# One shift of a value tile by one key: four partition ranges in place of two

## The chip, the cores and the metric

The kernel runs on one core of a Trainium2 chip. A core has TensorE (PE, with its weight loads PEld), VectorE (DVE), ScalarE (ACT), GpSimd (POOL), SyncE (SP) and 16 DMA engines, which move data between the chip's main memory and the on-chip memory of 128 partitions, or within the latter. The metric is the device time of one execution in microseconds, lower is better; each figure is a median of several executions.

## What is computed

Three blocks in a row on `x` of 512 tokens by 1024: a gated delta-rule layer, an attention layer with stick-breaking weights, and a block of a Fourier mixer beside dilated window attention. The change touches the second one. For each of 16 heads of width 64, with keys `k_sh` and values `v_sh`:

```
logits = einsum("bhtd,bhsd->bhts", q, kb) * Dh ** -0.5
mask = s_idx[None, :] < t_idx[:, None]
log_keep = where(mask, log_sigmoid(-logits), 0.0)
after = sum(log_keep, -1, keepdims=True) - cumsum(log_keep, -1)
wts = where(mask, exp(log_sigmoid(logits) + after), 0.0)
outs.append(einsum("bhts,bhsd->bhtd", wts, vb))
```

The kernel doesn't form `wts`. It runs a scan over the keys and multiplies its result by differences of neighbouring values, `v[s] - v[s-1]`. So each value row is needed once more, moved down by one key.

## The kernel before

All instructions of each engine are written out by hand in program order; nothing reorders them. Engines meet at semaphores only.

**Weights.** A dense product is cut into blocks of 512 output columns (`blocks`), a block into two halves `s`. SP loads a half (1 MB, 128 partitions) into `raw[:, s, :]` at L549. ACT rounds it into `whi` (L782), POOL subtracts the rounded part from `raw` and leaves the rest in `wlo` (L608), and PE computes hi·hi, lo·hi and hi·lo (L2072), three groups of 8 matmuls for each of the four output tiles of a block, two tiles to a half. The three products stand in for one of higher precision. There are two slots of `raw`, so SP may load a half of the next block only when POOL has finished with that of the block before (`raw_free` waits on `lo_ready`). The wait stands on SP, and everything that is written behind it on SP waits too.

**The stretch around the change.** The order of the blocks is `D_VB`, `D_VB + 1` (values, written by ACT into `Vb` at L1162 and L1146), `D_QB`, `D_QB + 1` (queries), `D_ZB`, `D_ZB + 1` (gate), then the attention. The names are indices of blocks. `Vb` is 128 partitions by `NT` = 4 by 1024 floats, token `128 * j + p` in partition `p` and row `j`; that is 16 KB in each partition.

**The shift.** Just ahead of the load of `D_ZB`, SP waits until `Vb` is complete and issues two transfers from `Vb` to `v_down`: partitions 0 to 126 go to partitions 1 to 127 (L590, 2032 KB), and partition 127 of rows 0 to 2 goes to partition 0 of rows 1 to 3 (L591, 12 KB). POOL clears the first key (L708). After both halves of `D_ZB` are split, POOL waits for `v_shifted` and subtracts `v_down` from `Vb` in four instructions (L713). The first reader of the differences is the attention, at L2710.

**What PE, ACT and DVE do at the same time.** For the queries, ACT squares each finished tile (L787), PE sums the squares over each head (`head_sums`, L2236), ACT takes the root (`root_pair`: L808, L809, L810, then L812, L814 into `rbuf`) and DVE scales (L1766). A `head_sums` waits until ACT has read the sums of the pair before (`ss_read`, counted up at L808 and L810). In ACT's program the rounding of the first half of `D_ZB` (`next_hi(D_QB + 1, 0)`) stands ahead of `roots(G_QB, SQ_QB)`. DVE copies finished query tiles out of the PSUM banks (L1756), which frees these banks for the tiles of `D_ZB`. ACT takes the gate tiles out at L1180 and L1185.

The five lines of PE's program in this stretch, in words: `dense_block(D_QB)`, `dense_unit(D_QB + 1, 0)`, a `head_sums`, `dense_unit(D_QB + 1, 1)` with a second `head_sums` between its two tiles, then the units of `D_ZB` in the same manner.

Of the kernel before, what the change touches and what calls it, by code (L numbers as in the profile page):

```python
# [104 lines left out]
def mixer_stack(nc, x, c, norm_g, w_ada, b_ada, w_in_a, conv_w_a, a_log_a, dt_bias_a, o_gain_a, w_out_a,  # L105
# [3 lines left out]
    with ctx:  # L109
        def sb(name, shape, dt=F32, scope=None):  # L110
            return (scope or ctx).enter_context(nc.sbuf_tensor(name, shape, dt))
# [99 lines left out]
        with ExitStack() as B:  # L211
# [4 lines left out]
            with ExitStack() as s2:  # L216
                v_down = sb("v_down", [128, NT, D], F32, s2)
# [15 lines left out]
            Vb = sb("Vb", [128, NT, D], F32, B)  # L233
# [74 lines left out]
        def raw_ch(s):  # L308
            return raw[:, s, :].rearrange("p (k n) -> p k n", k=KD)

        def spare(what, n):

            return what == "ada" and (n - EARLY) % 2 == 1
# [8 lines left out]
        def late_src(n, s):  # L322
            return late_w[:, s, :].rearrange("p (k n) -> p k n", k=KD) if spare("ada", n) else raw_ch(s)
# [15 lines left out]
        def early(u):  # L339

            return (ada_a if u % EARLY < 2 else ada_b)[:, u % 2 + 2 * (u // EARLY), :].rearrange("p (k n) -> p k n", k=KD)

        halves = [sum(kind == "t" for _, _, kind in blocks[:d]) for d in range(len(blocks))]

        def unit_used(eng, d, s):
# [9 lines left out]
        def unit(buf, s, kind):  # L355
            return buf[:, s, :].rearrange("p (k n) -> p k n", k=KD if kind == "ch" else KD // 2)
# [79 lines left out]
        def v_stage(n):  # L436

            return (pT2 if n in (6, 7) else yst if n in (2, 3, 10, 11) else vst)[:, n % 2, :]
# [86 lines left out]
        @block.sync  # L525
        def _(sp):
            def raw_free(r, s):

                of = [load for load in order[:r] if spare(*load) == spare(*order[r])]
                if not of:  # L530
                    sp.wait_ge(dense_full, 4 * D_OUTA)
                    return
                what, n = of[-1]
                sp.wait_ge(ada_done if what == "ada" else lo_ready, 2 * n + s + 1)

            def load(r, halves=(0, 1)):
                what, n = order[r]
                for s in halves:
                    if r:
                        raw_free(r, s)  # L540
                    if what == "dense" and blocks[n][2] == "t":
                        w, col, _ = blocks[n]
                        src = w[512 * s:512 * s + 512, col:col + 512].rearrange("(k p) n -> p k n", p=128)
                        dst = unit(raw, s, "t")
                    else:
                        w, col = ada[n] if what == "ada" else blocks[n][:2]
                        src = w[:, col + 256 * s:col + 256 * s + 256].rearrange("(k p) n -> p k n", p=128)
                        dst = late_src(n, s) if what == "ada" else raw_ch(s)
                    sp.dma_start(dst, src).then_inc((ada_loaded if spare(what, n) else raw_loaded)[s], 16)  # L549

            for i in range(NT):
                sp.dma_start(xnat[:, i, :], x[0, 128 * i:128 * i + 128, :]).then_inc(x_tile[i], 16)
            load(0, (0,))
            sp.wait_ge(rows_loaded, 16 * 13)
            for o, u in enumerate(EARLY_ORDER):
                if o == 2:
                    load(0, (1,))
                sp.dma_start(early(u), w_ada[0][:, 256 * u:256 * u + 256].rearrange("(k p) n -> p k n", p=128)
                             ).then_inc(ada_loaded[u], 16)
            sp.dma_start(cs[:, N_FIRST:N_CST], cst[:, N_FIRST:N_CST]).then_inc(cst_loaded, 16)  # L560
            with sp.Fori(1, 6) as i:
                for s in range(2):
                    sp.wait_ge(lo_ready, i * 2 + (s - 1))
                    src = w_in_a[0][:, bass.ds(i * 512 + 256 * s, 256)].rearrange("(k p) n -> p k n", p=128)
                    sp.dma_start(raw_ch(s), src).then_inc(raw_loaded[s], 16)
            def v_moves(n0, moves):

                for t in range(NT):
                    n = n0 + t
                    sp.wait_ge(v_done, 8 + n + 1)  # L570
                    for dst, src in moves(t, v_stage(n)):
                        sp.dma_start(dst, src).then_inc(v_moved[n % 2], 16)

            def moves_a(t, src):
                return [(vA[64:128, t, :], src[0:64, :]), (vA[0:64, t + 1, :], src[64:128, :])]

            def moves_b(cfg):
                return lambda t, src: [(vB[32 * t:32 * t + 32, r, cfg, :], src[r:128:4, :]) for r in range(NCLS)]

            for r in range(load_of["dense", 6], len(order)):  # L580
                if r == load_of["dense", D_VA2 + 2]:
                    sp.wait_ge(va_zero, 2)
                    v_moves(0, moves_a)
                if r == load_of["dense", D_VB2 + 2]:
                    sp.wait_ge(n_done, 4)
                    v_moves(4, moves_b(0))
                if r == load_of["dense", D_ZB]:
                    sp.wait_ge(v_done, 8)
                    sp.wait_ge(dense_full, 4 * (D_VB + 2))
                    sp.dma_start(v_down[1:128, :, :], Vb[0:127, :, :]).then_inc(v_shifted, 16)  # L590
                    sp.dma_start(v_down[0:1, 1:NT, :], Vb[127:128, 0:NT - 1, :]).then_inc(v_shifted, 16)  # L591
                load(r)
                if r == load_of["dense", D_VB2 + 2]:
                    v_moves(8, moves_b(1))
            sp.dma_start(picks_raw[:, :, :, :], pick.rearrange("a (n h m) -> a n h m", n=2, h=4)).then_inc(fc_loaded, 16)
            for b in range(2):
                for t in range(NT):
                    sp.wait_ge(out2_done, 4 * b + t + 1)
                    sp.dma_start(out[0, 128 * t:128 * t + 128, 512 * b:512 * b + 512],
                                 qB[:, 4 * b + t, :]).then_inc(stored, 16)  # L600
            sp.wait_ge(stored, 16 * 2 * NT)
# [3 lines left out]
        def _(pool):  # L605
            def split_lo(d, s):
                pool.wait_ge(hi_ready, 2 * d + s + 1)
                pool.tensor_tensor(wlo[:, s, :], raw[:, s, :], whi[:, s, :].bitcast(F32),  # L608
                                   ALU.subtract).then_inc(lo_ready, 1)
# [93 lines left out]
            for d in range(D_OUTA + 1, D_OUTB):  # L703
                for s in range(1 if d in own_parts else 2):
                    split_lo(d, s)
                if d == D_VB + 1:
                    pool.wait_ge(dense_full, 4 * (D_VB + 2))
                    pool.memset(v_down[0:1, 0, :], 0.0).then_inc(v_diff, 1)  # L708
                if d == D_ZB:
                    pool.wait_ge(v_diff, 1)  # L710
                    pool.wait_ge(v_shifted, 32)
                    for j in range(NT):
                        pool.tensor_tensor(Vb[:, j, :], Vb[:, j, :], v_down[:, j, :], ALU.subtract).then_inc(v_diff, 1)  # L713
            split_lo(D_OUTB, 0)
# [2319 lines left out]
```

## Time and profile before

| | us |
|---|---|
| median of 3 executions | 1237.84 (1235.95 to 1239.93) |
| profiled execution, its own time | 1238.93 |
| its span, first to last instruction | 1236.9 |
| PE busy | 1126.8 (91%) |
| PE weight loads busy | 887.0 (72%) |
| ACT busy | 520.1 (42%) |
| DVE busy | 498.2 (40%) |
| POOL busy | 381.3 (31%) |
| mean granted TensorE clock | 0.964 of full |

The program moves 119.37 MB by DMA, nearly all of it weights (the queue of SP and ACT, `q1` in the profile). The profile's views used here: the span in 40 slices (a digit is the busy share in tenths), the waits of an engine, the chain of work that ended last, the timelines of single engines, the view of one source line with its transfers' times from issue to landing, and sums over chosen stretches. Start times count from the span's start. A matmul's end is modelled, so starts of neighbours tell more than durations.

### The profile page before, as it was taken

The page shows a single profiled execution, that of the slowest core. Times are in us where ns is not written, and L with a number is a line of the kernel's source. Part 1 is how long each engine was busy: PE and PEld are TensorE (multiplying, and loading weights), DVE is VectorE, ACT ScalarE, POOL GpSimd, SP SyncE. Part 2 cuts the span into 40 slices and gives each one's busy share as a digit, 9 for nine tenths or more (in the row PEclk, how much of TensorE's full clock was granted, in tenths as well). Part 3 has the DMA queues.
Part 4 walks back from the last instruction along what each step waited for, and adds up shares of the span by engine and source line. Part 5 has one row for each costly group of instructions (what it writes and reads, how often), then busy time and mean ns, then how long its engine had stood idle before and what let it go on. Part 6 is the DMA issues. An engine that isn't in the chain of part 4 may idle for free.

```text
span 1236.9 us, 21346 instructions
## 1 busy us (share of the span) xinstructions
PE 1126.8 (91%) x8978; PEld 887.0 (72%) x8978; DVE 498.2 (40%) x889; ACT 520.1 (42%) x911; POOL 381.3 (31%) x153
## 2 busy tenths in 40 slices
PE   5999999999899999989018999999999999999998
PEld 4788876677678888767016766788887777678777
DVE  4575544544324382330013188284302333221553
ACT  4232237634246254531025488343324543653540
POOL 0143343132165214433016310123344222433161
PEclk8999999999999999989559999999999999999999
DMA  9723331486620222230212210132232512233301
GB/s 314 231 69 102 102 102 35 144 266 212 204 70 11 94 69 103 68 103 27 88 36 87 68 35 1 35 102 86 69 119 69 145 43 69 68 102 130 112 1 68
DMA packets 102976, 119.37 MB, mean 97 GB/s; under 512 B 4649, under 2 KB 89177, under 8 KB 102761
## 3 DMA queue, kind: packets, MB, share of 16 engines
q1 hardware_dynamic: 99024, 115.08, 28.8%
q10 hardware_dynamic: 3864, 3.01, 0.8%
q8 instruction: 68, 1.11, 0.4%
q14 instruction: 20, 0.16, 0.0%
HBM read 110.75 MB, written 2.10 MB: 91 GB/s over the span
## 4 chain that ended last, share of the span: by engine, by line
PE 77%; ACT 6%; another core or an unknown queue 5%; DVE 5%; issue 4%; DMA 1%; ACTq 0%; SPq 0%; POOL 0%; DVEq 0%
PE ps L2072 39%; PE ps L2865 4%; PE ps L2118 2%; PE ps L2213 2%; PE ps L2460 2%; PE ps L2675 2%; PE ps L2710 2%; PE ps L2156 1%; PE ps L2693 1%; PE ps L2831 1%; PE ps L2289 1%; PE ps L2487 1%; PE ps L2236 1%; PE ps L2818 1%
## 5 line engine op out<-in xcount | busy, mean ns | idle before, releaser
L608 POOL TENSOR_TENSOR wlo<-raw,whi 128x2048 fp32r<-128x2048 f32 x53 | 245.2, 4627 | 573.0 <-ACT whi L782 560.6
L782 ACT ACTIVATE whi<-raw 128x2048 fp32r<-128x2048 f32 x52 | 99.3, 1911 | 260.3 <-PE ps L2072 153.1
L614 POOL TENSOR_TENSOR wlo<-raw,whi 128x2048 fp32r<-128x2048 f32 x10 | 46.4, 4641 | 111.4 <-ACT whi L871 62.7
L2236 PE MATMUL ps<-work,cs 64*64 64x512 f32 x160 | 22.7, 637 | 57.0 <-ACT rbuf L810 57.0
L1802 DVE TENSOR_TENSOR_SCAN taken<-kept,taken 128x255 f32<-128x255 f32 (+2 forms) x64 | 51.2, 853 | 34.2 <-ACT taken L1202 34.1
L1292 ACT ACTIVATE p<-sc,nmx 128x256 f32<-128x256 f32 x64 | 32.0, 501 | 45.8 <-PE ps L2818 44.7
L1766 DVE SCALAR_TENSOR_TENSOR qTb<-qTb,qcol,rbuf 128x512 f32<-128x512 f32 x8 | 12.7, 1623 | 93.9 <-ACT rbuf L812 93.9
L2236 PEld LDWEIGHTS ps<-work,cs 64*64 64x64 f32 x160 | 4.4, 135 | 63.9 <-issue 63.1
L1899 DVE CUSTOM_DVE_ANT_0 sc<-ps,biast 128x256 f32<-128x256 f32 (+1 forms) x64 | 22.5, 393 | 65.8 <-PE ps L2807 36.7
L2072 PE MATMUL ps<-hC_hi,whi 128*128 128x512 f32 x184 | 47.0, 398 | 0.8 <-POOL wlo L608 0.8
L871 ACT ACTIVATE whi<-raw 128x2048 fp32r<-128x2048 f32 x11 | 21.1, 1917 | 62.7 <-PE ps L2072 62.7
L2072 PE MATMUL ps<-hC_lo,whi 128*128 128x512 f32 x184 | 45.5, 390 | 0.0
L2072 PE MATMUL ps<-hC_hi,wlo 128*128 128x512 f32 x184 | 45.5, 389 | 0.0
L2072 PEld LDWEIGHTS ps<-hC_hi,whi 128*128 128x128 f32 x184 | 33.7, 188 | 14.8 <-issue 6.4
L2072 PE MATMUL ps<-hB_hi,whi 128*128 128x512 f32 x120 | 35.1, 441 | 9.0 <-issue 5.6
L2072 PEld LDWEIGHTS ps<-hC_lo,whi 128*128 128x128 f32 x184 | 34.6, 188 | 7.4
L2072 PEld LDWEIGHTS ps<-hC_hi,wlo 128*128 128x128 f32 x184 | 34.6, 188 | 7.1
L2072 PE MATMUL ps<-hA_hi,whi 128*128 128x512 f32 x160 | 39.5, 389 | 0.0
L2072 PE MATMUL ps<-hA_hi,wlo 128*128 128x512 f32 x160 | 39.5, 390 | 0.0
L2072 PE MATMUL ps<-hA_lo,whi 128*128 128x512 f32 x160 | 39.5, 390 | 0.0
L2072 PEld LDWEIGHTS ps<-hB_hi,whi 128*128 128x128 f32 x120 | 25.1, 215 | 19.2 <-issue 13.8
L1470 DVE SCALAR_TENSOR_TENSOR work<-ps,cols,work 128x511 f32<-128x511 f32 (+1 forms) x48 | 36.0, 750 | 6.1 <-DVE work L1467 0.2
(506 smaller groups left out, 2714.9 us busy)
## 6 DMA issues: line engine op xcount, KB each, us to landing
raw<-in_w_in_dram SPq DMA_DIRECT2D x24, 1024.0 KB, 5.2
raw<-in_w_in_a_dram SPq DMA_DIRECT2D x16, 1024.0 KB, 5.6
raw<-in_w_ada_dram SPq DMA_DIRECT2D x8, 1024.0 KB, 5.1
late_w<-in_w_ada_dram SPq DMA_DIRECT2D x8, 1024.0 KB, 5.5
raw<-in_w_kv_dram SPq DMA_DIRECT2D x8, 1024.0 KB, 5.2
raw<-in_w_in_b_dram SPq DMA_DIRECT2D x8, 1024.0 KB, 5.6
ada_a<-in_w_ada_dram SPq DMA_DIRECT2D x4, 1024.0 KB, 9.9
ada_b<-in_w_ada_dram SPq DMA_DIRECT2D x4, 1024.0 KB, 13.2
```

The costliest lines, as they stand in the source:

```text
L608: pool.tensor_tensor(wlo[:, s, :], raw[:, s, :], whi[:, s, :].bitcast(F32), ALU.subtract).then_inc(lo_ready, 1)
L614: pool.tensor_tensor(wlo[:, s, :], raw[:, s, :], whi[:, s, :].bitcast(F32), ALU.subtract).then_inc(lo_ready, 1)
L782: A(whi[:, s, :], raw[:, s, :], ACT.Copy).then_inc(hi_ready, 1)
L1292: A(p2[:, n % 2, 256 * e:256 * e + 256], sc2[:, n % 2, 256 * e:256 * e + 256], ACT.Exp, scale=-1.0, bias=nmx[:, grp, t, 2 * hp + e:2 * hp ...
L1470: STT(y[:, n:], src[:, 0:T - n], tap(3 - n), y[:, n:], ALU.mult, ALU.add).then_inc(conv_step, 1)
L1802: last = dve.tensor_tensor_scan(taken[:, r % 3, keys], kept[:, r % 3, keys], taken[:, r % 3, keys], 0.0, ALU.mult, ALU.add)
L2072: last = mm(out, l[a], r[b], start=start and at == 0, stop=stop and at == n - 1)
L2118: last = mm(dense[m][:, cols], w[:, k, 128 * (m % 2):128 * (m % 2) + 128], x[:, k, cols], start=half == 0 and q == 0, stop=stop and q == 2 ...
L2213: last = mm(modrow(2 * EARLY)[32 * (k % 4):32 * (k % 4) + 32, :], cactz[:, k, 23 - n:55 - n], late_src(a, s)[:, k, :], start=n == 0 and k ...
L2236: last = mm(ssbank(g + tile)[to, :], ones[of, 0:64], work4[of, (n + tile) % 4, :], start=True, stop=True)
L2460: last = mm(block64(0, s, i, 1 - n), ntm[side(n), (2 * p + s) % 4, i, :], xin[side(n), (2 * p + s) % 4, i, :], start=True, stop=True)
L2865: last = mm(dense[2 * s + m], w[:, k, 128 * m:128 * m + 128], x[:, k, :], start=q == 0, stop=q == 23)
```

## The change

The first of the two transfers is written as three, over partitions 0 to 111, 112 to 119 and 120 to 126; the one of partition 127 stays as it is. POOL waits for 64 in place of 32, since each of the four transfers adds 16. The bytes moved, the place in SP's program and all else are the same.

```
                     sp.wait_ge(v_done, 8)
                     sp.wait_ge(dense_full, 4 * (D_VB + 2))
-                    sp.dma_start(v_down[1:128, :, :], Vb[0:127, :, :]).then_inc(v_shifted, 16)
+                    sp.dma_start(v_down[1:113, :, :], Vb[0:112, :, :]).then_inc(v_shifted, 16)
+                    sp.dma_start(v_down[113:121, :, :], Vb[112:120, :, :]).then_inc(v_shifted, 16)
+                    sp.dma_start(v_down[121:128, :, :], Vb[120:127, :, :]).then_inc(v_shifted, 16)
                     sp.dma_start(v_down[0:1, 1:NT, :], Vb[127:128, 0:NT - 1, :]).then_inc(v_shifted, 16)
...
-                    pool.wait_ge(v_shifted, 32)
+                    pool.wait_ge(v_shifted, 64)
```

## Rows read from the trace of the kernel before

**Rows 1.** The page, span in 40 slices of 30.9 us: granted TensorE clock

```profile
PEclk8999999999999999989559999999999999999999
```

**Rows 2.** Waits of PE, whole span: line, releaser: total us, times, longest

```profile
PE ps L2236 <- ACT rbuf L810: 57.0, 4, 56.5
...
PE ps L2072 <- ACT zsT L1180: 3.4, 1, 3.4
```

**Rows 3.** Chain that ended last, 560 to 680 us: start, length, what

```profile
580.59 59.13 another core or an unknown queue
```

**Rows 4.** Timeline of SP: start, length, line, operation, tiles, count

```profile
550.43 0.37 SPq L549 DMA_DIRECT2D raw<-in_w_in_b_dram  x1
550.90 0.80 SPq L590 DMA_DIRECT2D v_down<-Vb  x1
551.77 36.88 SPq L591 DMA_DIRECT2D v_down<-Vb  x1
...
588.69 9.60 SPq L549 DMA_DIRECT2D raw<-in_w_in_b_dram  x2
```

**Rows 5.** Line L549, loads issued in 550:551, then in 590:593

```profile
DMA to landing us min/median/max: 5.3/5.3/5.3
...
DMA to landing us min/median/max: 50.7/50.8/51.0
```

**Rows 6.** Stretches: engines' busy us (instructions), granted clock, DMA share, GB/s

```profile
548.00:550.00 2.00, 2.00 (x8) 1.53 (x6) 0.00 (x0) 0.00 (x0) 2.00 (x1) 0.62 1.05 370
...
556.00:558.00 2.00, 2.00 (x11) 1.65 (x10) 0.00 (x0) 0.00 (x0) 0.00 (x0) 1.00 0.06 25
...
612.00:614.00 2.00, 0.00 (x0) 0.00 (x0) 0.00 (x0) 0.00 (x0) 0.00 (x0) 0.50 0.06 25
...
642.00:644.00 2.00, 0.23 (x4) 0.26 (x8) 0.00 (x0) 1.94 (x4) 2.00 (x1) 0.50 0.00 0
```

**Rows 7.** Timeline of ACT; the bracket is idle time before and its releaser

```profile
639.74 1.91 ACT L782 ACTIVATE whi<-raw 128x2048 fp32r<-128x2048 f32 x1 [67.03 <-DMA raw<-in_w_in_b_dram]
...
642.95 0.68 ACT L810 ACTIVATE rbuf<-ps,cs 64x512 f32<-64x512 f32 x1
...
653.51 1.90 ACT L782 ACTIVATE whi<-raw 128x2048 fp32r<-128x2048 f32 x1
...
663.79 1.91 ACT L782 ACTIVATE whi<-raw 128x2048 fp32r<-128x2048 f32 x1 [7.34 <-PE ps L2072]
```

**Rows 8.** Timeline of PE (matmuls), 8 matmuls to a row

```profile
580.46 1.09 PE L2236 MATMUL ps<-work,cs 64*64 64x512 f32 x8
...
585.26 1.98 PE L2072 MATMUL ps<-hB_hi,wlo 128*128 128x512 f32 x8
643.77 1.99 PE L2236 MATMUL ps<-work,cs 64*64 64x512 f32 x8 [56.54 <-ACT rbuf L810]
...
652.61 2.02 PE L2072 MATMUL ps<-hB_hi,whi 128*128 128x512 f32 x8
...
663.62 1.09 PE L2236 MATMUL ps<-work,cs 64*64 64x512 f32 x8
...
670.32 1.09 PE L2236 MATMUL ps<-work,cs 64*64 64x512 f32 x8
...
680.51 3.75 PE L2072 MATMUL ps<-hB_hi,whi 128*128 128x512 f32 x8 [3.41 <-ACT zsT L1180]
684.06 2.94 PE L2072 MATMUL ps<-hB_lo,whi 128*128 128x512 f32 x8
```

**Rows 9.** Timelines of DVE (first two rows) and POOL (last two)

```profile
651.66 2.48 DVE L1756 COPY qTb<-ps 128x512 f32<-128x512 f32 x4
...
668.38 6.71 DVE L1766 SCALAR_TENSOR_TENSOR qTb<-qTb,qcol,rbuf 128x512 f32<-128x512 f32 x2 [14.25 <-ACT rbuf L812]
...
560.87 4.64 POOL L608 TENSOR_TENSOR wlo<-raw,whi 128x2048 fp32r<-128x2048 f32 x1 [10.47 <-ACT whi L782]
...
660.09 9.46 POOL L713 TENSOR_TENSOR Vb<-Vb,v_down 128x1024 f32<-128x1024 f32 x4
```

## Prediction

> **What bounds the kernel now.** Start with the page: TensorE is busy for 91% of the span, and its granted clock is near full in all slices but three in the middle [rows 1]. Next, the waits of PE. One stands out: a `head_sums` (L2236) waited for ACT's L810 for 57.0 us in four waits, 56.5 of it in one [rows 2]. The next one of interest is 3.4 us. A releaser is only the last link, so ask what ACT waited for. ACT's timeline says: the rounding of the first half of `D_ZB` (L782) started at 639.74 after 67.03 us idle, released by the DMA into `raw` [rows 7]. L810 stands behind it on ACT, and PE behind L810. The chain that ended last has the same hole: 59.13 us from 580.59 for which it knows only an unknown queue [rows 3]. So the question is why that load came so late.
>
> SP's timeline answers in part. The last load ahead of the shift went out at 550.43, the large shift transfer at 550.90 in 0.80 us, but the small one sat on SP from 551.77 for 36.88 us, so both loads of `D_ZB` went out only from 588.69 [rows 4]. And then they took 51 us to land, where the load issued at 550.43 took 5.3 [rows 5]. The stretches show what was going on: from 556 to 558 and from 612 to 614 us the DMA share is 0.06, one part in 16, at 25 GB/s, where with all engines at work it is 1.05 at 370 GB/s [rows 6]. One of 16 engines works, the rest are idle; by 642 it is over. The shift holds 2044 KB, 2.09 MB; at 25 GB/s that is 84 us, and from 551.8 to 639.7 there are 88 in which this engine also carries its shares of three loads. So the 127-partition transfer runs on a single DMA engine, each load behind it needs that engine for its own share (a load ends when its slowest share ends), and SP itself is held since that engine's queue is full.
>
> The Trainium skill, "DMA: Bandwidth & Descriptors", section "Why a DMA increments its semaphore by 16 and not by 1", has the rule for this: the number of engines is the largest one up to 16 that divides the slowest dimension of both sides, so 127 partitions go to one engine; the trace agrees by its share of 0.06 [rows 6]. By it 112 partitions take 16 engines, 8 take 8 and 7 take 7; no row here shows these three sizes.
>
> **The change, part by part.**
>
> 1. The 112 partitions. 112 x 16 KB is 1.84 MB. The upper bound of their time is one engine at 25 GB/s, 73 us; the lower bound is all at 370 GB/s, 5.0 us [rows 6]. I take 5.0: the loads of 128 partitions are the nearest row in shape, 112 is a multiple of 16 as 128 is, and 127 is a multiple of nothing.
>
> 2. The 8 and the 7 partitions. If each partition goes to an engine of its own, 16 KB at 25 GB/s is 0.7 us each. If all 15 go to one engine, 0.25 MB is 9.8 us. I take 1.3 for both and keep 9.8 as the bound.
>
> 3. Issue on SP. Between 0.37 us (a load) and 0.80 us (the large transfer) for each [rows 4], some 1 us more for two transfers added; the 36.88 goes, since no engine has a long backlog. These issues are hidden: after them SP waits anyway for POOL to free the slot, which is L608 at 560.87 plus 4.64, so 565.5 [rows 9]. The load ahead of the shift lands at 550.43 + 5.3 = 555.7. With 5.0 + 1.3 behind it the shift is over at about 562, and with 9.8 in place of 1.3 at 570.5.
>
> 4. The load of `D_ZB`, first half. Issued at 565.5, landed 5.3 later, at 570.8; in the bad case of step 3 at about 576. ACT wants it when PE has finished the second tile of `D_QB + 1`. At the same place a block later ACT starts 0.17 us after the `head_sums` (663.79 against 663.62) [rows 7, 8], so here at 580.46 + 0.17 = 580.63. Ten us to spare, 5 in the bad case. ACT's row moves from 639.74 to 580.63: **59.1 us earlier**.
>
> 5. What is late next. L810 ended at 642.95 + 0.68 = 643.63 [rows 7], now at 584.5. PE wants it for its second `head_sums`. One `head_sums` and one tile at full clock take 670.32 - 663.62 = 6.70 us [rows 8], so PE gets there at 587.16 and does not wait. The last query tile is done another 6.70 later, at 593.86, where `D_ZB` begins. It began at 652.61 [rows 8]: **58.75 us earlier**. Less than 59.1 because PE now has to do its own work in order, although the restart at half clock (1.99 for a `head_sums`, not 1.09 [rows 8]; clock 0.50 [rows 6]) is saved as well. For that start PE needs a free bank, so DVE's first copy of L1756. The four start at 651.66 and take 2.48 [rows 9]; 59.1 earlier the first ends at about 593.2, 0.7 before PE wants it. This is the tightest spot. If it is late by as much again, that costs 0.7.
>
> 6. POOL's subtraction (L713) started at 660.09 [rows 9] and moves to 601. The shift is over some 30 us before, also in the bad case, so the wait for 64 costs nothing. ACT's second rounding of `D_ZB` (653.51 [rows 7]) and POOL move by 59.1 with step 4. From 663 on the order of everything repeats with a common shift. The wait of PE before 680.51 for ACT's L1180 stays: behind it is DVE's L1766 at 668.38, 6.71 us for two [rows 9], which overlaps POOL's work and moves with POOL or with PE. So the shift of all that follows is between 58.75 and 59.1; I take 59.0.
>
> No later wait depends on an absolute time: loads are issued when a slot is freed, by the work before them.
>
> **The sum.** Span 1236.9 - 59.0 = 1177.9. Profiled execution 1238.93 - 59.0 = 1179.9. That execution lies 1.1 above the median of 1237.84, so the median should become 1178.8.
>
> **Rivals.**
>
> *A, the clock.* After 3.4 us idle PE restarted at 680.51 slowly: groups of 3.75 and 2.94 us in place of 1.98 [rows 8], 2.7 us lost. What it does there may depend on the idle stretch 36 us before, which goes. If the loss there goes as well, 1176.1. For it: nothing but that dependence. Against: at 548 the clock is also partly low (0.62) after a wait that came with no long hole before [rows 6]. The other way, one such restart more costs 2.7: 1181.5.
>
> *B, the 112 are not spread.* If they too go to one engine, the bytes on that engine are the same and so is the hole: 1237.8, no difference. The Trainium skill's "Rules for kernel authors" in "DMA: Bandwidth & Descriptors" speak against the change on their face: many small transfers should be merged, and two transfers over disjoint partition ranges bring nothing, since both use the same engines. Read so, the result would be B's. But that presumes that the one transfer is spread already, and a share of 0.06 says it is not [rows 6].
>
> *C, spread in part.* The transfer must be off the engines by 580.63 - 5.3 = 575.3, so 19.6 us after 555.7. At 25 GB/s an engine moves 0.49 MB in this, a fourth of 1.84: four engines are enough. With two it takes 36.7 us, the load lands near 597.7, 42 us earlier than now, and the time is 1195.8.
>
> *D, slower.* The 36.88 us on SP is a price of each transfer behind the first, not of the backlog. Then three such issues hold SP from 551.77 to 662.4, the load lands at 667.7 in place of 639.7, and the time is 1265.8. It decides from 28.8 us each: then the load lands 3.7 us later than now, which is 0.3%. For it: SP did stand for 36.88 with a 12 KB transfer. Against: 36.88 us at 25 GB/s is 0.92 MB, near half of the large one, so it looks like room made in a queue; and with nothing before them loads are issued in 0.37 [rows 4].
>
> **How the numbers follow.** The forecast 0.82, A 0.11 (both ways), C 0.02, B 0.03, D 0.02. The executions before spread by 2 us to either side. The range takes A both ways and that spread: 1176.1 - 2 = 1174 below, 1181.5 + 2 = 1183.5 above, which also holds the 0.7 of step 5. Faster by over 0.3% (3.7 us, about what a measurement of this kernel can tell from no change): forecast, A and C, 0.95. Same: B, 0.03. Slower: D, 0.02.
>
> **What would show it.** SP's loads of `D_ZB` at about 565.5 and 576.4, each landed in 5 to 6 us. DMA share from 556 to 562 near 1, not 0.06. ACT's L782 at 580.6, released by PE and not by DMA. No wait of PE for L810 above 1 us. The tile of `D_ZB` at 593.9, L713 near 601, and the same waits as before behind it, 59 us earlier; PE's clock at 1.00 from 590 to 620. I am wrong if SP still stands for tens of us behind L590, if one engine's share lasts beyond 575, or if a wait of PE of more than 3 us turns up between 587 and 650.

## The result and the profile after

The changed kernel takes 1180.67 us (median, 1178.48 to 1185.62) against 1238.58 for the kernel before in the same comparison: a ratio of 0.954, 95% interval 0.951 to 0.958. A second comparison on another chip, `e9_changed_again` below, gave 0.952 (0.951 to 0.954). The forecast was 1178.8 in a range of 1174 to 1183.5. The profiled execution took 1180.23 with a span of 1178.2, so 58.7 us of span less; 59.0 had been worked out.

From L593 on line numbers are two higher than before: L608 is now L610, L782 is L784, L713 is L715, L810 is L812, L1180 is L1182, L1756 is L1758, L1766 is L1768, L2072 is L2074 and L2236 is L2238. First the page: the two slices at 5 tenths of the clock in the middle are gone (compare [rows 1]; two slices at 8 remain), and PE is busy for 95% of the span.

```profile
PE 1123.5 (95%) x8978; PEld 883.7 (75%) x8978; DVE 496.7 (42%) x889; ACT 520.1 (44%) x911; POOL 381.6 (32%) x153
...
PEclk7899999999999999998999999999999999999999
```

PE's waits: the one of 56.5 us for L810 ([rows 2]) is no longer among them; what stood behind it in the list comes first now.

```profile
PE ps L2074 <- issue: 5.6, 1, 5.6
PE ps L2256 <- DMA cs<-in_cst_dram: 4.9, 1, 4.9
PE ps L2228 <- DMA ada_a<-in_w_ada_dram: 4.3, 3, 3.0
PE ps L2074 <- ACT zsT L1182: 3.3, 1, 3.3
```

SP's timeline (start, length), the answer to [rows 4]. The four transfers hold SP for 4.7 us in all, not 37.7, and the first load of `D_ZB` goes out at 566.82, when POOL has freed the slot.

```profile
551.39 1.43 SPq L590 DMA_DIRECT2D v_down<-Vb  x1
552.87 0.77 SPq L591 DMA_DIRECT2D v_down<-Vb  x1
553.70 0.78 SPq L592 DMA_DIRECT2D v_down<-Vb  x1
554.51 1.73 SPq L593 DMA_DIRECT2D v_down<-Vb  x1
566.82 36.02 SPq L549 DMA_DIRECT2D raw<-in_w_in_b_dram  x4
```

The two loads of `D_ZB` (issued in 566:568 and in 577:578) landed in about 6 us, where it was 51 ([rows 5]):

```profile
DMA to landing us min/median/max: 6.1/6.1/6.1
...
DMA to landing us min/median/max: 5.6/5.6/5.6
```

The stretches (last three columns: granted clock, DMA share, GB/s), beside [rows 6]. The shift has all engines up to about 561, half of the share to 564, and then it is nearly silent. The clock from 612 to 614 is 1.00, where it was 0.50.

```profile
556.00:558.00 2.00, 2.00 (x10) 1.65 (x10) 0.00 (x0) 0.00 (x0) 0.00 (x0) 1.00 1.08 288
558.00:560.00 2.00, 2.00 (x11) 1.65 (x10) 0.00 (x0) 0.00 (x0) 0.00 (x0) 1.00 1.07 319
...
562.00:564.00 2.00, 2.00 (x11) 1.65 (x10) 0.00 (x0) 1.10 (x3) 1.85 (x1) 1.00 0.48 83
564.00:566.00 2.00, 2.00 (x10) 1.66 (x9) 0.47 (x1) 0.00 (x0) 2.00 (x1) 1.00 0.03 3
...
612.00:614.00 2.00, 2.00 (x13) 0.80 (x12) 2.00 (x2) 0.00 (x0) 2.00 (x1) 1.00 0.00 0
```

ACT, PE and POOL beside [rows 7 to 9]. ACT's rounding of `D_ZB` at 581.91 is now released by PE (after 7.92 us idle) and not by the DMA; PE's second `head_sums` at 588.44 has no wait; the first tile of `D_ZB` starts at 595.05.

```profile
581.91 1.91 ACT L784 ACTIVATE whi<-raw 128x2048 fp32r<-128x2048 f32 x1 [7.92 <-PE ps L2074]
...
581.74 1.09 PE L2238 MATMUL ps<-work,cs 64*64 64x512 f32 x8
...
588.44 1.09 PE L2238 MATMUL ps<-work,cs 64*64 64x512 f32 x8
...
595.05 1.98 PE L2074 MATMUL ps<-hB_hi,whi 128*128 128x512 f32 x8
...
622.83 3.30 PE L2074 MATMUL ps<-hB_hi,whi 128*128 128x512 f32 x8 [3.34 <-ACT zsT L1182]
625.93 2.39 PE L2074 MATMUL ps<-hB_lo,whi 128*128 128x512 f32 x8
...
602.40 9.47 POOL L715 TENSOR_TENSOR Vb<-Vb,v_down 128x1024 f32<-128x1024 f32 x4
```

### The profile page after: what moved, and what is told of

It reads as the page before. It is cut to its first block, busy times and chain, and to the rows that moved or that the text cites. A ratio compares the mean times of both kernels' runs of the same rounds, so it can differ in the third digit from the quotient of the medians.

```text
span 1178.2 us, 21348 instructions
## 1 busy us (share of the span) xinstructions
PE 1123.5 (95%) x8978; PEld 883.7 (75%) x8978; DVE 496.7 (42%) x889; ACT 520.1 (44%) x911; POOL 381.6 (32%) x153
## 4 chain that ended last, share of the span: by engine, by line
PE 82%; ACT 7%; DVE 5%; issue 4%; DMA 1%; SPq 1%; ACTq 0%; POOL 0%; DVEq 0%
PE ps L2074 42%; PE ps L2867 4%; PE ps L2120 2%; PE ps L2462 2%; PE ps L2215 2%; PE ps L2677 2%; PE ps L2712 2%; PE ps L2158 1%; PE ps L2695 1%; PE ps L2291 1%; PE ps L2833 1%; PE ps L2489 1%; PE ps L2238 1%; PE ps L2820 1%; DMA ada_a<-in_w_ada_dram 1%
## 5 line engine op out<-in xcount | busy, mean ns | idle before, releaser
L610 POOL TENSOR_TENSOR wlo<-raw,whi 128x2048 fp32r<-128x2048 f32 x53 | 245.4, 4632 | 514.2 <-ACT whi L784 501.8
L784 ACT ACTIVATE whi<-raw 128x2048 fp32r<-128x2048 f32 x52 | 99.3, 1911 | 202.0 <-PE ps L2074 160.9
L2074 PE MATMUL ps<-hC_hi,whi 128*128 128x512 f32 x184 | 46.9, 397 | 0.8 <-POOL wlo L610 0.8
L2074 PE MATMUL ps<-hC_lo,whi 128*128 128x512 f32 x184 | 45.5, 390 | 0.0
L2074 PE MATMUL ps<-hC_hi,wlo 128*128 128x512 f32 x184 | 45.4, 389 | 0.0
L2074 PEld LDWEIGHTS ps<-hC_hi,whi 128*128 128x128 f32 x184 | 33.7, 188 | 14.8 <-issue 6.4
L2074 PE MATMUL ps<-hB_hi,whi 128*128 128x512 f32 x120 | 33.3, 424 | 8.9 <-issue 5.6
L2074 PEld LDWEIGHTS ps<-hC_lo,whi 128*128 128x128 f32 x184 | 34.5, 188 | 7.4
L2074 PEld LDWEIGHTS ps<-hC_hi,wlo 128*128 128x128 f32 x184 | 34.5, 188 | 7.2
L2074 PE MATMUL ps<-hA_lo,whi 128*128 128x512 f32 x160 | 39.5, 389 | 0.0
L2074 PE MATMUL ps<-hA_hi,wlo 128*128 128x512 f32 x160 | 39.5, 389 | 0.0
L2074 PE MATMUL ps<-hA_hi,whi 128*128 128x512 f32 x160 | 39.5, 389 | 0.0
L2074 PEld LDWEIGHTS ps<-hB_hi,whi 128*128 128x128 f32 x120 | 23.8, 203 | 17.8 <-issue 12.9
L1592 DVE COPY_PREDICATED yib<-cs,ps 128x256 f32<-128x256 int32 x20 | 10.0, 501 | 59.9 <-PE ps L2462 59.9
L625 POOL COPY yib<-cs 128x512 f32<-128x512 f32 x20 | 12.6, 630 | 70.1 <-PE ps L2490 70.1
L2074 PEld LDWEIGHTS ps<-hA_hi,wlo 128*128 128x128 f32 x160 | 30.0, 188 | 6.2
```

The costliest lines, as they stand in the source:

```text
L784: A(whi[:, s, :], raw[:, s, :], ACT.Copy).then_inc(hi_ready, 1)
L2074: last = mm(out, l[a], r[b], start=start and at == 0, stop=stop and at == n - 1)
```

## The experiments

**My theory:** the 127 partitions ran on one of 16 DMA engines, and each load behind them had to wait for that engine. **The rivals:** it is the hold of SP by the small transfer, not the engine; or only multiples of 16 are spread; or the number and the kind of the transfers matter by themselves. All differences below are against the changed kernel, except where said.

### The number of engines as a dose: 122, 123, 124, 126 partitions

The count of partitions sets the number of engines in my theory, so other splits of the same 127 give two, three, four and 14.

```
-                    sp.dma_start(v_down[1:113, :, :], Vb[0:112, :, :]).then_inc(v_shifted, 16)
-                    sp.dma_start(v_down[113:121, :, :], Vb[112:120, :, :]).then_inc(v_shifted, 16)
-                    sp.dma_start(v_down[121:128, :, :], Vb[120:127, :, :]).then_inc(v_shifted, 16)
+                    sp.dma_start(v_down[1:123, :, :], Vb[0:122, :, :]).then_inc(v_shifted, 16)
+                    sp.dma_start(v_down[123:128, :, :], Vb[122:127, :, :]).then_inc(v_shifted, 16)
...
-                    pool.wait_ge(v_shifted, 64)
+                    pool.wait_ge(v_shifted, 48)
```

The others differ in the bounds alone (123 and 4, 124 and 3, 126 and 1, each with the transfer of partition 127 as it was).

> The shift as 122, 5 and 1 partitions. My theory (a transfer's partitions are dealt out over as many engines as the largest divisor of their count up to 16, and the load behind waits for the slowest of them): 122 = 2 x 61 runs on two engines, DMA share 0.12 to 0.13 once the load ahead has landed, 1.0 MB each at 25 to 28 GB/s, over at 592 to 596. The first half of D_ZB lands at 595 to 599, ACT rounds it then, 16 us later than in the changed kernel: 1193 to 1197 us. Rival, any count but a multiple of 16 goes to one engine: 1238. Rival, only the odd count 127 is bad: 1180.

> The shift as 123, 4 and 1 partitions. My theory: 123 = 3 x 41 runs on three engines, share 0.19, 0.67 MB each, 24 to 27 us, over at 580 to 583; the load lands at 585 to 588, 4 to 7 us after ACT could have used it; most of it reaches PE, 2 to 5 us over the changed kernel: 1182 to 1186. Rival, not a multiple of 16 means one engine: 1238. Rival, only even counts are dealt out: 1238.

> The shift as 124, 3 and 1 partitions. My theory: four engines, share 0.25, 0.51 MB each, over at 574 to 576, the load lands at 580 to 582, just in time: 1180 to 1181, the same as the changed kernel within its noise, with the wait of PE for the second head_sums under 1 us. It is the point from which the number of engines decides. Rival, one engine: 1238.

> The shift as 126, 1 and 1 partitions. My theory: 126 runs on 14 engines, nine partitions each, over at 562 or so, 1179 to 1182, the same as the changed kernel with one transfer less. Rival, only multiples of 16 are spread: 1238 (one engine) or 1196 (two).

Measured medians: 1199.55, 1189.47, 1190.78 (1187.26 to 1198.98, the widest of them) and 1182.31 us. The stretch from 557 to 566 us of the first three shows the engines at work: shares 0.13, 0.19 and 0.25, two, three and four parts in 16.

```profile
557.00:566.00 9.00, 9.00 (x41) 7.44 (x41) 1.38 (x2) 2.96 (x3) 4.20 (x1) 1.00 0.13 55
...
557.00:566.00 9.00, 9.00 (x41) 7.47 (x40) 0.69 (x1) 2.95 (x3) 2.66 (x1) 1.00 0.19 82
...
557.00:566.00 9.00, 9.00 (x42) 7.44 (x41) 1.38 (x2) 2.96 (x3) 4.64 (x1) 1.00 0.25 75
```

In each the wait of PE is the one of before, only shorter: for the root behind ACT's rounding of `D_ZB` (here L811), 17.4 us on two engines, 4.4 on three, 7.6 on four, none above 0.2 on 14. Timelines of PE of the three, in that order:

```profile
605.52 1.98 PE L2237 MATMUL ps<-work,cs 64*64 64x512 f32 x8 [17.36 <-ACT rbuf L811]
...
594.07 1.81 PE L2237 MATMUL ps<-work,cs 64*64 64x512 f32 x8 [4.36 <-ACT rbuf L811]
...
594.68 1.99 PE L2237 MATMUL ps<-work,cs 64*64 64x512 f32 x8 [7.63 <-ACT rbuf L811]
```

PE's wait falls as the rate of the shift rises: 28 GB/s before, then 55, 75 (four engines), 82 (three) and 341 (14). So that the shift sat on few engines is shown to be the cause; what each engine moves counts beside their number. "Multiples of 16 alone" has fallen: 126 partitions do as well as 112. The Trainium skill's rule in "DMA: Bandwidth & Descriptors", section "Why a DMA increments its semaphore by 16 and not by 1" (the largest number up to 16 that divides the partitions), gives exactly these counts, and the shares agree. The times for two and three engines lie 2.6 and 3.5 us above my ranges. Two things were missing there. The load behind has a share on the same engines and landed later than said, 35.0 us and 22.0 us after its issue, at 601.5 and 590.0 (said 595 to 599 and 585 to 588). And PE restarts slowly behind its wait: from this `head_sums` to the first tile of `D_ZB` it takes 8.7 us in all three, where the changed kernel takes 6.6, so even a short wait costs about 2 us more than its length. The expectation for four was wrong by 10 us, and that mainly for a reason of its own: the four engines moved 75 GB/s, 19 each, where one, two and three moved 27 to 28 each. The last two runs below ask about that.

### The engine or the hold of SP: the 127 from ACT's queue

```
+            act.wait_ge(v_done, 8)
+            act.dma_start(v_down[1:128, :, :], Vb[0:127, :, :]).then_inc(v_shifted, 16)
...
-                    sp.dma_start(v_down[1:113, :, :], Vb[0:112, :, :]).then_inc(v_shifted, 16)
-                    sp.dma_start(v_down[113:121, :, :], Vb[112:120, :, :]).then_inc(v_shifted, 16)
-                    sp.dma_start(v_down[121:128, :, :], Vb[120:127, :, :]).then_inc(v_shifted, 16)
...
-                    pool.wait_ge(v_shifted, 64)
+                    pool.wait_ge(v_shifted, 32)
```

The first two lines stand behind ACT's last copy into `Vb`.

> The transfer of 127 partitions as before, but issued by ACT when its values are written; SP issues only the one of partition 127, and so is never held. Tells the hold on SP from the one busy engine. My theory: the loads of D_ZB go out on time at 565 and 576 from another queue, share the busy engine with the shift, and land 3 to 8 us later than with it free, in time for PE; but the shift itself still ends at about 635 to 645, so POOL's subtraction, which stood at 602, waits for it, and what is queued behind on POOL, the low part of D_ZB + 1, with it. PE waits 30 to 40 us for that: 1210 to 1220. Rival, the hold of SP alone is the cost: 1180. Rival, the busy engine serves its queues one after the other: 1238.

Measured: 1241.09 us, a ratio of 1.000 (0.998 to 1.003) to the kernel before. "The hold of SP alone" has fallen. But my number has fallen too: the engine was not shared evenly. Now the two loads of `D_QB + 1`, issued at 545.8 and 550.3, were the victims: they landed 50.7 and 82.1 us later, and SP was held by its 12 KB all the same. PE waited twice, for the low parts that hang on them. The time is also that of the rival of queues served one after the other, but the landings speak against it: alone, the large transfer, issued at 541.0, needs 2.08 MB at 26 GB/s, 80 us, and the first load landed at 596.5, well before that. SP's timeline, the landings of the two loads, the packets of each queue from 540 to 640 us, and PE's two waits:

```profile
550.82 39.96 SPq L590 DMA_DIRECT2D v_down<-Vb  x1
603.01 0.39 SPq L549 DMA_DIRECT2D raw<-in_w_in_b_dram  x1
...
DMA to landing us min/median/max: 50.7/66.4/82.1
...
q1 hardware_dynamic: 3152, 3.16, 10.3%
q10 hardware_dynamic: 128, 2.08, 5.3%
...
603.04 3.78 PE L2073 MATMUL ps<-hB_hi,whi 128*128 128x512 f32 x8 [32.67 <-POOL wlo L607]
639.03 3.78 PE L2073 MATMUL ps<-hB_hi,whi 128*128 128x512 f32 x8 [20.98 <-POOL wlo L607]
```

`q10` is ACT's queue: 128 packets for 2.08 MB, 16 KB each. `q1` is SP's alone, not that of SP and ACT as I wrote ahead of the prediction: 3152 for 3.16 MB, 1 KB each. An estimate: if the busy engine takes one packet of each queue in turn, the 64 packets of a load's share need 64 x 17.4 KB at 26 GB/s, 43 us for each of the two loads and 86 for both. The first took 50.7 from its issue, and both were there 86.6 us after it. The rule of the Trainium skill in "DMA: Bandwidth & Descriptors", section "Queues, rings and completion order", is this turn by packets, and the landings agree with it. That each engine really alternates was not seen packet by packet. Here, then, a second queue did not protect small rows from a long transfer with large rows.

### The order of the two transfers of before

```
-                    sp.dma_start(v_down[1:113, :, :], Vb[0:112, :, :]).then_inc(v_shifted, 16)
-                    sp.dma_start(v_down[113:121, :, :], Vb[112:120, :, :]).then_inc(v_shifted, 16)
-                    sp.dma_start(v_down[121:128, :, :], Vb[120:127, :, :]).then_inc(v_shifted, 16)
                     sp.dma_start(v_down[0:1, 1:NT, :], Vb[127:128, 0:NT - 1, :]).then_inc(v_shifted, 16)
+                    sp.dma_start(v_down[1:128, :, :], Vb[0:127, :, :]).then_inc(v_shifted, 16)
...
-                    pool.wait_ge(v_shifted, 64)
+                    pool.wait_ge(v_shifted, 32)
```

> The two transfers of before, the small one first. My theory: SP is not held by the small one, but the load of D_ZB behind the large one meets the same full queue: it is held, or lands late; 1236 to 1240, ACT's rounding again near 639. Rival, it is the small transfer behind the large one (1 partition, or its 36.88 us on SP) that costs: 1180 to 1205.

Measured: 1240.34 us, a ratio of 0.999 (0.997 to 1.002) to the kernel before. Neither transfer of the shift holds SP now (0.64 and 0.74 us); the first load of `D_ZB` does instead, for 21.6 us, and it lands 74.4 us after its issue. Line L549 in the stretch 564:570, and ACT's timeline:

```profile
L549 SPq DMA_DIRECT2D raw<-in_w_in_b_dram x1: 21555/21555/21555, 565.0 to 565.0; - x1
...
DMA to landing us min/median/max: 74.4/74.4/74.4
...
639.48 1.91 ACT L782 ACTIVATE whi<-raw 128x2048 fp32r<-128x2048 f32 x1 [67.30 <-DMA raw<-in_w_in_b_dram]
```

SP is let go at 586.6 here and at 588.7 before, whichever instruction stands behind the large one. The hold belongs to the backlog, not to the small transfer; rival D of the prediction has fallen.

### One whole transfer

```
-                    sp.dma_start(v_down[1:113, :, :], Vb[0:112, :, :]).then_inc(v_shifted, 16)
-                    sp.dma_start(v_down[113:121, :, :], Vb[112:120, :, :]).then_inc(v_shifted, 16)
-                    sp.dma_start(v_down[121:128, :, :], Vb[120:127, :, :]).then_inc(v_shifted, 16)
-                    sp.dma_start(v_down[0:1, 1:NT, :], Vb[127:128, 0:NT - 1, :]).then_inc(v_shifted, 16)
+                    sp.dma_start(v_down[:, :, :], Vb[:, :, :]).then_inc(v_shifted, 16)
...
-                    pool.wait_ge(v_shifted, 64)
+                    pool.wait_ge(v_shifted, 16)
```

This kernel leaves out the shift by one key: each value row is copied onto its own partition, so its output is not that of the layer. It serves for the time alone.

> One transfer of all 128 partitions onto the same partitions, with no shift by a key: the output leaves out the shift, and the differences in the attention are of a value with itself. The transfer is 16 KB longer. My theory: 16 engines, over at 561, 1179 to 1182, the same as the changed kernel: what costs is the count, not the number of transfers. If the four issues on SP (4.7 us) or the crossing of partitions cost anything, this is faster than the changed kernel by it, at most 2 us.

Measured: 1180.95 us, a ratio of 0.953 (0.948 to 0.958) to the kernel before, the time of the changed kernel. No cost of three more transfers, or of crossing partitions, shows in the time. The transfer itself went faster: over five us (556 to 561) 444 GB/s at a share near 1, where the changed kernel shows 277 in its eight us (555 to 563). First the whole one, then the changed kernel:

```profile
556.00:561.00 5.00, 5.00 (x24) 4.13 (x23) 0.69 (x1) 1.10 (x1) 0.00 (x0) 1.00 1.05 444
...
555.00:563.00 8.00, 8.00 (x37) 6.63 (x36) 1.03 (x2) 2.85 (x3) 0.85 (x1) 1.00 0.98 277
```

### Using the early shift: POOL's subtraction moved up

The largest wait left behind the change is PE's 3.3 us for ACT's L1182, with DVE's two slow L1768 (6.63 us) behind it, while POOL works on the low part that its four subtractions had pushed back. Since the shift ends so early now, these can move into POOL's idle time. DVE and POOL in the changed kernel:

```profile
610.78 6.63 DVE L1768 SCALAR_TENSOR_TENSOR qTb<-qTb,qcol,rbuf 128x512 f32<-128x512 f32 x2 [14.35 <-ACT rbuf L814]
...
611.82 5.04 POOL L610 TENSOR_TENSOR wlo<-raw,whi 128x2048 fp32r<-128x2048 f32 x1
```

```
                 for s in range(1 if d in own_parts else 2):
                     split_lo(d, s)
+                    if d == D_QB + 1:
+                        if s == 0:
+                            pool.wait_ge(v_diff, 1)
+                            pool.wait_ge(v_shifted, 64)
+                        for j in range(2) if s == 0 else range(2, NT):
+                            pool.tensor_tensor(Vb[:, j, :], Vb[:, j, :], v_down[:, j, :], ALU.subtract).then_inc(v_diff, 1)
...
-                if d == D_ZB:
-                    pool.wait_ge(v_diff, 1)
-                    pool.wait_ge(v_shifted, 64)
-                    for j in range(NT):
-                        pool.tensor_tensor(Vb[:, j, :], Vb[:, j, :], v_down[:, j, :], ALU.subtract).then_inc(v_diff, 1)
```

> The changed kernel with POOL's four subtractions moved up: two after the low part of the first half of D_QB + 1 (POOL is free from 566.8 to 573.0), two after that of the second half (577.7 to 583.9). The shift is over at 562, which the two transfers of before never allowed. POOL then has nothing between 602 and 608, and the low part of D_ZB + 1 runs from 608.1 to 612.7 in place of 611.8 to 616.9, beside less of DVE's L1768 (6.6 us for two where alone it is 1.4). So DVE ends some 2 to 4 us earlier, the wait of PE for ACT's L1182 (3.3 us) goes to 0 to 1.5, and the slow restart behind it (1.7 us) with it: 1175 to 1178, a gain of 3 to 5 over the changed kernel. Rival: the time of L1768 is its own and not from POOL: no gain, 1180.

Measured: 1175.75 us, a ratio to the kernel before of 0.947 (0.944 to 0.950). The low part runs at 607.04 in 4.63 us, the two L1769 take 3.25 in place of 6.63, and PE goes from `D_ZB` to `D_ZB + 1` without a wait and without a slow restart. POOL, DVE and PE:

```profile
566.52 4.76 POOL L713 TENSOR_TENSOR Vb<-Vb,v_down 128x1024 f32<-128x1024 f32 x2 [0.88 <-DMA v_down<-Vb]
...
607.04 4.63 POOL L610 TENSOR_TENSOR wlo<-raw,whi 128x2048 fp32r<-128x2048 f32 x1 [5.74 <-ACT whi L785]
...
609.63 3.25 DVE L1769 SCALAR_TENSOR_TENSOR qTb<-qTb,qcol,rbuf 128x512 f32<-128x512 f32 x2 [14.34 <-ACT rbuf L815]
...
618.30 2.08 PE L2075 MATMUL ps<-hB_hi,whi 128*128 128x512 f32 x8
```

The first of these rows also dates the end of the shift: POOL waited for it until 566.5.

### The same with 126, beside the changed kernel

`e9_changed_again` is the changed kernel itself. `e10_early_126` has the moved subtraction and the bounds of `e4_126_on_fourteen`.

> The changed kernel as it is, beside the next one on the same chip: 1178 to 1183. It gives the yardstick for the gain of the earlier subtraction, which so far was compared over the kernel before alone.

> The earlier subtraction with the shift as 126, 1 and 1 partitions. In the run with 112, 8, 7 and 1 POOL waited at last for the shift, which was complete at 566.5 only, 4 us after my step; the 112 moved at 210 to 280 GB/s at a DMA share near 1, where the 126 on 14 engines moved at 330 to 410. My theory: the shift is complete 2 to 3 us earlier, POOL starts its subtraction right behind the low part at about 565.7, and since POOL had 0.6 us to spare there, the time does not move: 1173 to 1177, 4 to 6 below the changed kernel. Rival: the wait of POOL cost up to 0.9 us: 1172 to 1176.

Measured on one chip, five executions of each: 1180.50 and 1176.02 us, ratios to the kernel before of 0.952 (0.951 to 0.954) and 0.948 (0.947 to 0.950). The intervals do not overlap: 4.5 us for the moved subtraction and the 126 together. The 126 alone gained nothing (1182.31 in `e4_126_on_fourteen`), and the moved subtraction alone reached 1175.75, so I put the gain down to the move. POOL no longer waits for the shift (L712 starts at 567.17, as L609 ends), and, as expected, the time did not move for it. The best of these kernels stands near 1176.

### What slows four engines: 125 and 119 partitions

> The shift as 125, 2 and 1 partitions, five engines, 0.41 MB each. On one, two and three engines each moved 26 to 28 GB/s, on four 19 only, and that run came out at 1190 where I had said 1180. If 26 GB/s each holds, the shift is over at 572 and the load lands in time: 1179 to 1183. If some 78 GB/s in total is a limit for few engines, it takes 26 us, over at 582, the load lands at 587 to 590: 1186 to 1191, with a wait of PE for the second head_sums of 3 to 7 us.

> The shift as 119, 8 and 1 partitions, seven engines, 0.28 MB each. At 26 GB/s each it is over at 567: 1179 to 1183, no wait of PE. If some 78 GB/s in total is a limit for few engines: 25 us, 1186 to 1190. If the rate falls with each engine's range of partitions cutting across those of others (17 partitions each), 15 to 19 GB/s each, over at 571 to 574, just in time: 1179 to 1184, but a total of 105 to 135 GB/s in the stretch from 557 to 566 and not 180.

Their edits are again the bounds alone (125 and 2; 119 and 8). Measured: 1181.49 and 1179.11 us, neither with a wait of PE for the root above 0.2 us. The stretch 557:566 of both:

```profile
557.00:566.00 9.00, 9.00 (x42) 7.44 (x41) 0.69 (x1) 2.96 (x3) 2.60 (x1) 1.00 0.32 135
...
557.00:566.00 9.00, 9.00 (x41) 7.46 (x40) 1.38 (x2) 2.96 (x3) 4.64 (x1) 1.00 0.43 137
```

The table takes these two and all others from the same view, in stretches in which only the shift runs (about; the last two begin with the tail of the load ahead, and the one of 112 holds the small transfers of 8, 7 and 1 too; from 557 on they moved 266 and 422 GB/s, 17 and 26 each):

| partitions / engines | partitions each | share | GB/s | GB/s each |
|---|---|---|---|---|
| 127 / 1 (before) | 127 | 0.07 | 28 | 28 |
| 122 / 2 | 61 | 0.13 | 55 | 27 |
| 123 / 3 | 41 | 0.19 | 82 | 27 |
| 124 / 4 | 31 | 0.25 | 75 | 19 |
| 125 / 5 | 25 | 0.32 | 135 | 27 |
| 119 / 7 | 17 | 0.43 | 137 | 20 |
| 126 / 14 (557 to 562) | 9 | 0.87 | 341 | 24 |
| 112 / 16 (555 to 563) | 7 | 0.98 | 277 | 17 |
| 128 / 16, no shift (556 to 561) | 8 | 1.05 | 444 | 28 |

A limit of 78 GB/s in total for few engines has fallen: five moved 135. Three splits are slow in each engine, with 31, 17 and 7 partitions to an engine, and one lies a little below the rest, with 9. That is what the runs show; what slows an engine there is open. It was not tried with a range that starts elsewhere.

## Why the prediction was right

The time of 1180.67 lies in the range, and the way there went as written, step by step; two sizes on it were wrong and cost nothing.

- **What bounds the kernel.** One busy engine of 16, and the load of `D_ZB` behind it, is now shown and not only read: one, two, three and four engines gave 1238, 1199.6, 1189.5 and 1190.8 us, five, seven and 14 gave 1181.5, 1179.1 and 1182.3, and changing the queue or the order gave nothing.
- **Steps 1 and 2, the size of the transfers.** Mis-sized: 5.0 us for the 112 partitions came from the rate of loads, 370 GB/s. The eight us from 555 to 563 show 277. With the tail of the small ones the shift was complete at 566.5 in `e8_early_subtraction`, whose first transfer went out at 550.39, half a us ahead of the kernel before; I had said 562. It cost nothing, since its reader stood at 602.
- **Step 3, the issue on SP.** Mis-sized as well: 4.7 us for four, where 0.80 each at most, 3.2, had been said. Hidden as said: SP next waited for POOL, to 566.8.
- **Step 4, the load.** Forecast in this execution's time: the stretch up to `head_sums` runs 1.28 us later than before (581.74, not 580.46), half a us from earlier in the program, the rest from a restart at 546 that stayed slow longer (clock 0.50 from 548 to 550, not 0.62). With that added: ACT at 581.91, said 580.63 + 1.28 = 581.91. Landed at 572.9, 9 us ahead; 10 were said.
- **Step 5, what is late next.** PE's second `head_sums` at 588.44, said 587.16 + 1.28 = 588.44. First tile of `D_ZB` at 595.05, said 593.86 + 1.28 = 595.14. DVE's first copy of L1758 was done at about 594.6, half a us ahead, so the tightest spot held.
- **Step 6, the rest moves together.** POOL's subtraction at 602.40, said 601 + 1.28 = 602.3. PE behind ACT's L1182 at 622.83, said 680.51 - 59.0 + 1.28 = 622.79.
- **The sum.** 1.28 later, and 1.0 won back at the restart of 622.83 (groups of 3.30 and 2.39 us, not 3.75 and 2.94): 58.7 where 59.0 was said. That the two nearly cancel was luck. The median lies 1.9 above the forecast: 0.3 is this error; the rest is that the profiled execution before lay 1.1 above its median, and this one lies 0.4 below.

**The rivals.** A: the slow restart stayed, at 1.7 in place of 2.7 us, so a part of it came. The other traces repeat this: the two groups lose 2.7 and 2.6 us in the two kernels with the wait of 56 us (before, `e6_small_first`) and 1.6 to 1.8 us in the changed kernel and the nine others where the wait for L1182 stands. `e5_127_on_act_queue`, with two shorter waits of PE in place of the one, is among the nine, so an idle stretch alone does not make the difference; what does is not shown. B: fallen. C: its mechanism is real, as 122, 123 and 124 show; but its threshold, "four engines are enough", was wrong, since it took 25 GB/s for each engine and four moved 19. Five were enough. Its price for two, 1195.8, was 3.8 too low: it had the load at 597.7 and no slow restart. D: fallen with the changed kernel itself, where the three transfers behind the first hold SP for 3.3 us, and with `e6_small_first`.

## What to carry to other kernels

Look at the partition count of each transfer, above all for a large prime number next to a stream of loads: a DMA share of one sixteenth in the stretches and a load that lands tens of us late are its mark, even where the transfer itself is not waited for. Cut it into ranges whose counts have a divisor of 16 or little less; the extra transfers cost SP under 2 us each. Another queue did not help here: the loads' shares stood on the same engine, beside larger packets. And when a transfer ends 70 us earlier, look at who could now use its result earlier: here that was worth another 4.5 us.

## What the runs showed of the hardware that I had not expected

- A transfer in one queue delays those in another on the same engine: beside 16 KB packets from ACT's queue, two loads in 1 KB packets landed after 50.7 and 82.1 us, not 5.3.
- SP stood 39.96 us at a 12 KB transfer though the large one was on ACT's queue and not its own.
- The rate of an engine in a copy within the on-chip memory differed with the number of partitions that each engine got: 26 to 28 GB/s at 8, 25, 41, 61 and 127, 24 at 9, 17 to 20 at 7, 17 and 31. Why is open.
- DVE's two L1768 took 6.63 us with POOL at work beside them for 6.1 of it, 3.25 (L1769 in `e8_early_subtraction`) where POOL's low part ended 1.2 us before they did, and 1.41 with POOL idle (the next two, in both).
